# Four stages of a small hybrid decoder on one core: table loads, a gate bank, meta scores and one turn reordered, unused products put into waits

## What the reference computes

```python
u = rmsnorm(h); proj = u @ w_in[l]                 # -> cq 384, ckv 256, kr 32, xr 512, gt 512
q = rmsnorm(rmsnorm(cq) @ w_uq); k, v = rmsnorm(ckv) @ w_ukv ...   # 8 heads, 64 + 32 rotary
att = causal softmax attention                     # blocks of queries: 16 meta, 128, 128
rnn = rglru(conv4(xr)) * gelu(gt)                  # sigmoid gates by w_a, w_i, then a scan
h = h + concat(rmsnorm(att), rmsnorm(rnn)) @ w_out[l]
h = h + (swiglu(rmsnorm(h)) if l == 0 else top-2-of-8 mixture of swiglu experts)
```

## Time and profile before

| what | value |
|---|---|
| median of 3 runs | 895.87 us (894.41 to 896.41) |
| the profiled execution | 898.03 us, its span 896.2 us |
| busy | PE 866.8 us (97%), DVE 683.6, ACT 576.0, POOL 70.8 |
| mean granted clock | 0.985 of full speed |

### The profile page before, as it was taken

How to read it: one execution, slowest core, us unless ns; L and a number is a source line. 1 busy time by engine, 2 the same in 40 slices (tenths; PEclk the granted TensorE clock), 3 DMA queues, 4 the chain that set the end, 5 groups by cost and what they waited for, 6 DMA issues and landing times.

```text
span 896.2 us, 15435 instructions
## 1 busy us (share of the span) xinstructions
PE 866.8 (97%) x5827; PEld 794.5 (89%) x5827; DVE 683.6 (76%) x914; ACT 576.0 (64%) x782; POOL 70.8 (8%) x93
## 2 busy tenths in 40 slices
PE   8989899999999999999899999999999999999995
PEld 7855789999999999965799989999998989999994
DVE  5667867766666555677877889789897998789883
ACT  6666746555454443666746777787778777777762
POOL 3530010000000000000042000000000000000001
PEclk9999899999999999999999999999999999999998
DMA  9505025555578553405055799899998999899981
GB/s 314 189 2 185 17 95 165 173 179 187 167 199 240 144 170 112 142 19 170 13 206 182 261 362 371 324 348 404 345 405 302 372 391 361 314 353 402 353 346 26
DMA packets 119436, 208.70 MB, mean 233 GB/s; under 512 B 5968, under 2 KB 71760, under 8 KB 119376
## 3 DMA queue, kind: packets, MB, share of 16 engines
q1 hardware_dynamic: 117232, 201.79, 63.7%
q0 software_dynamic: 1568, 5.24, 2.9%
q10 hardware_dynamic: 576, 0.87, 0.4%
HBM read 202.65 MB, written 5.24 MB: 232 GB/s over the span
## 4 chain that ended last, share of the span: by engine, by line
PE 85%; DVE 6%; ACT 4%; DMA 3%; issue 2%; POOL 0%; ACTq 0%; DVEq 0%; POOLq 0%; SPq 0%
PE ps L2551 27%; PE ps L2576 12%; PE ps L668 11%; PE ps L670 11%; PE ps L669 10%; PE ps L2156 2%; PE ps L2516 2%; DVE wlo L1436 2%; PE ps L2263 2%; PE ps L2322 1%; DMA raw<-in_w_in_dram 1%; PE ps L2047 1%; PE ps L2563 1%; DMA raw<-in_moe_w_down_dram 1%; DVE rr L1453 1%
## 5 line engine op out<-in xcount | busy, mean ns | idle before, releaser
L1436 DVE TENSOR_TENSOR wlo<-raw,whi 128x1536 fp32r<-128x1536 f32 (+4 forms) x298 | 437.9, 1495 | 90.5 <-ACT whi L984 88.2
L984 ACT ACTIVATE whi<-raw 128x1536 fp32r<-128x1536 f32 (+4 forms) x298 | 374.7, 1275 | 128.6 <-PE ps L670 58.1
L668 PE MATMUL ps<-uhi,whi 128*128 128x272 f32 (+1 forms) x576 | 170.3, 296 | 0.6 <-DVE wlo L1436 0.6
L670 PE MATMUL ps<-uhi,wlo 128*128 128x272 f32 (+1 forms) x576 | 166.8, 290 | 0.0
L669 PE MATMUL ps<-ulo,whi 128*128 128x272 f32 (+1 forms) x576 | 166.5, 289 | 0.0
L2551 PE MATMUL ps<-whi,xeh 128*128 128x320 f32 (+1 forms) x512 | 125.0, 325 | 0.0
L2551 PE MATMUL ps<-whi,xel 128*128 128x320 f32 (+1 forms) x512 | 123.5, 322 | 0.0
L2551 PE MATMUL ps<-wlo,xeh 128*128 128x320 f32 (+1 forms) x512 | 123.5, 322 | 0.0
L668 PEld LDWEIGHTS ps<-uhi,whi 128*128 128x128 f32 (+1 forms) x576 | 109.0, 189 | 4.2 <-issue 2.2
L669 PEld LDWEIGHTS ps<-ulo,whi 128*128 128x128 f32 (+1 forms) x576 | 109.2, 190 | 0.6
L670 PEld LDWEIGHTS ps<-uhi,wlo 128*128 128x128 f32 (+1 forms) x576 | 108.9, 189 | 0.0
(11 more groups left out here) (314 smaller groups left out, 1200.3 us busy)
## 6 DMA issues: line engine op xcount, KB each, us to landing
raw<-in_moe_w_down_dram SPq DMA_DIRECT2D x24, 1536.0 KB, 9.2
raw<-in_moe_w_gate_dram SPq DMA_DIRECT2D x16, 1536.0 KB, 7.5
raw<-in_moe_w_up_dram SPq DMA_DIRECT2D x16, 1536.0 KB, 8.5
raw<-in_moe_w_gate_dram SPq DMA_DIRECT2D x16, 1280.0 KB, 10.1
raw<-in_moe_w_up_dram SPq DMA_DIRECT2D x16, 1280.0 KB, 9.4
raw<-in_ffn_w_gate_dram SPq DMA_DIRECT2D x11, 1024.0 KB, 5.2
raw<-in_ffn_w_up_dram SPq DMA_DIRECT2D x11, 1024.0 KB, 5.2
raw<-in_ffn_w_down_dram SPq DMA_DIRECT2D x8, 1408.0 KB, 6.9
```

The source lines that it names most:

```text
L668: pe.matmul(dst, wh, xh, start=start, stop=False, skip_group_check=True)
L670: return pe.matmul(dst, wl, xh, start=False, stop=stop, skip_group_check=True)
L984: act.activation(placed(whi, s, src), src, ACT.Copy).then_inc(hi_done, 1)
L1436: dve.tensor_tensor(placed(wlo, s, src), src, placed(whi, s, src).bitcast(F32), ALU.subtract).then_inc(lo_done, 1)
```

## The change

- Layer 1's gate block 3 gets bank 5, which was bank 7. Layer 0 keeps its banks.
- ACT's `tables()` and `mark(ACT.Tanh)` stand at the end of step xr 2, which was step xr 1.
- The meta scores of layer 0 go into one bank (6) as eight products side by side. DVE adds the mask, scales, takes the maximum and subtracts it, each for all heads in one instruction. ACT does one exponential for all heads, and `averages(0)` sums them on DVE. TensorE waits for the bank of gt 2 (bank 4) and puts two unused 128 x 128 products into it before heads 2, 4 and 6. Gate block 2 overwrites them.
- Three unused products stand before TensorE's wait at the query scales (`qrt`), in both layers, and the wait for the bank is ahead of them.
- In routing there are three unused products before the wait for `sel_done`, one before the wait for the norm, and two between the last two blocks of `hidden_state`. They go into bank 1.
- In the last expert DVE makes the low parts of the second turn between pieces 18 and 19. ACT's order stays as it was.

```diff
-GT_BANK = (6, 5, 4, 7)
+GT_BANK = ((6, 5, 4, 7), (6, 5, 4, 5))
...
-                for h in range(NH):
-                    add("s", t, h)
+                for h in range(NH if t else 1):
+                    add("s", t, h, bank=None if t else 6)
...
-                    if (name, c) == ("xr", 1):
+                    if (name, c) == ("xr", 2):
                         if not l:
                             tables()
                         mark(ACT.Tanh)
...
+                    if not t:
+                        s = scores[0][0:NMETA, :, 0:NMETA]
+                        act.activation(s, s, ACT.Exp).then_inc(exp_done, NH)
+                        return
...
+                def meta_maxima():
...
+                    dve.wait_ge(filled, b.ready())
+                    dve.tensor_tensor(s, ps[0:n, b.bank, 0:NH * n].rearrange("p (h k) -> p h k", h=NH), mask, ALU.add)                       .then_inc(emptied[b.bank], 1)
+                    dve.wait_ge(emptied[b.bank], b.before + 1)
+                    link(dve.tensor_tensor(s, s, of_head(rt[0:n, 0, :]), ALU.mult))
+                    link(dve.tensor_reduce(small[0:n, 0, 0, :], s, AX.X, ALU.max))
+                    dve.tensor_tensor(s, s, of_head(small[0:n, 0, 0, :]), ALU.subtract).then_inc(sc_done, 1)
...
+                    if not t:
+                        link(dve.tensor_reduce(small[0:n, 0, 2, :], scores[0][0:n, :, 0:n], AX.X, ALU.add))
...
-                    w(e, p, 18, 19)
-                    turned(6, TURN_B, 2)
+                    if is_last(e):
+                        w(e, p, 18)
+                        turned(6, TURN_B, 2)
+                        w(e, p, 19)
+                    else:
+                        w(e, p, 18, 19)
+                        turned(6, TURN_B, 2)
...
-                pe.wait_ge(rows_done, ROWS_DONE[l, "qk"])
                 b = B[l, "qrt"]
                 fill(pe, b)
+                for _ in range(3):
+                    pe.matmul(ps[:, b.bank, 0:P], ident, ident, start=True, stop=True, skip_group_check=True)
+                pe.wait_ge(rows_done, ROWS_DONE[l, "qk"])
...
+                def meta_scores():
...
+                    fill(pe, b)
+                    fill(pe, B[l, "gt", 2])
+                    for h in range(NH):
+                        if h in (2, 4, 6):
+                            unused(B[l, "gt", 2].bank, 2)
+                        kb = B[l, "kbc", h]
+                        pe.wait_ge(emptied[kb.bank], kb.before + 1)
+                        q = pe.matmul(ps[0:n, b.bank, n * h:n * (h + 1)], qT[0:QKH, h, 0:n], kT[0:QKH, h, 0:n],
+                                      start=True, stop=True)
+                    q.then_inc(filled, 1)
...
+            pe.wait_ge(emptied[spare.bank], spare.before + 1)
+            unused(3)
             pe.wait_ge(sel_done, 1)
...
+            unused(1)
             pe.wait_ge(nsum_done, KD - 2)
...
             hidden_state(0, 1)
+            unused(2)
             hidden_state(1, 1)
```

More of the change, by code:

```diff
@@ L260, in plan_blocks @@
             if what == "scores":
-                for h in range(NH):
-                    add("s", t, h)
+                for h in range(NH if t else 1):
+                    add("s", t, h, bank=None if t else 6)
             elif what == "gt":
-                add("gt", t, bank=GT_BANK[t])
+                add("gt", t, bank=GT_BANK[l][t])
             elif what == "meta":
@@ L1588, in _, with of_head @@
                 dve.wait_ge(qscale_done, l + 1)
+                def meta_maxima():
+                    n = NMETA
+                    m0 = C_MASK + T - P
+                    b = B[l, "s", 0, 0]
+                    s = scores[0][0:n, :, 0:n]
+                    mask = con[0:n, m0:m0 + n].rearrange("p (h k) -> p h k", h=1).to_broadcast([n, NH, n])
+                    def of_head(row):
+                        return row.rearrange("p (h k) -> p h k", k=1).to_broadcast([n, NH, n])
+                    dve.wait_ge(filled, b.ready())
[4 more added lines that the diff above has]
+                    dve.tensor_tensor(s, s, of_head(small[0:n, 0, 0, :]), ALU.subtract).then_inc(sc_done, 1)
                 def maxima(t):
                     lead, n = TILES[t]
+                    if not t:
+                        return meta_maxima()
                     keys = lead + n
@@ L2253, in _, with unused @@
                 pe.wait_ge(qrot_done, l + 1)
+                def meta_scores():
+                    n = NMETA
+                    b = B[l, "s", 0, 0]
+                    fill(pe, b)
[8 more added lines that the diff above has]
+                    q.then_inc(filled, 1)
+                def unused(bank, n):
+                    for _ in range(n):
+                        pe.matmul(ps[:, bank, 0:P], ident, ident, start=True, stop=True, skip_group_check=True)
                 def score(t):
                     lead, n = TILES[t]
+                    if not t:
+                        return meta_scores()
                     for h in range(NH):
@@ L2470, in hidden_state, with unused @@
                 q.then_inc(filled, 1)
+            spare = B[1, "wo", 5]
+            def unused(n):
+                for _ in range(n):
+                    pe.matmul(ps[:, spare.bank, 0:P], ident, ident, start=True, stop=True, skip_group_check=True)
             hidden_state(0, 0)
```

## The result

The changed kernel takes 887.98 us (median of 4 runs, 885.65 to 888.30) against 896.14 us before (4 runs beside it, 894.41 to 899.51): 8.2 us faster. The ratio, which is estimated from the single runs and not from the two medians, is 0.9890 (95% interval 0.9852 to 0.9928, which is 6.5 to 13.3 us). In a second comparison, some time later, it was 888.44 against 896.79 us, ratio 0.9919 (0.9897 to 0.9942). The profiled execution took 887.85 us, its span is 886.0 us, its mean granted clock 0.991.

The account below looks back on a forecast made before the run. TensorE, busy 97%, was taken as the bound, with time to win only in its idle, half-clock or off-chain places. Terms (a) to (h) summed to 9.0 us, off the median 895.87: 886.9 us, range 883.7 to 891.6.

Parts of the forecast that it names:

- (a): Layer 0 input stage: root ahead of the table loads, so DVE starts the reciprocal without its 1.79 us idle; 1.8 us won.
- (b): Layer 0, reciprocal to first query product: TensorE's gap shrinks to about 1.0 us and its clock stays up; 1.5 us won.
- (c): Recurrence gates, both layers: ACT's table load goes and TensorE closes its 1.07 us gap; 1.07 us each, 2.1 together.
- (e): Meta scores of layer 0: DVE starts later, but the tiles run at full clock; 0.7 us won, otherwise 0.8 lost.
- (g): Routing: gathers pushed back 0.6 us but taking 4.3 us at full clock; 0.4 us won, otherwise 0.6 to 1.2 lost.
- (h): Last expert's second turn: new DVE order wins 0.95 us, and the clock kept behind a 1.5 us gap 1.6; 2.55 together.
- (d): Query scales, both layers: three unused products take 0.7 us in a wait of 0.72; 0.1 us lost, bounds 0 and 1.4.
- (f): Gate block 3's bank, layer 1: TensorE's wait moves behind two transposes; value 0, bounds 0.3 us won and 1 lost.
- Unused products don't hold the clock: Rival: the clock falls at meta scores and routing, and behind the last turn's gap; gain 4.85 us, 891.0; chance 0.26.
- Transfers set the pace: Rival: the experts' transfers set their pace, earlier gains are lost and 2.55 us stay; 893.3 us; chance 0.07.
- A table load is put back: Rival: a load returns before the gates or the root, losing (c), or (a) with (b); 889 to 890.2 us; chance 0.06.
- Slower at half clock: Rival: unused products run at half clock and lengthen the path by 5.4 us; 896.4 to 897.7 us; chance 0.04.

Follow-up runs that it names:

- tables back: Changed kernel with the tables and tanh mark back at the end of step xr 1: 894.10 us, ratio to before 0.9966.
- no unused: Changed kernel without its 3 + 6 + 6 unused products, waits and banks kept: 890.29 us, ratio 0.9901.
- only tables: Kernel before with only the tanh mark and table work moved behind input block xr 2 instead of xr 1: 890.66 us, ratio 0.9925.

## Why the prediction was right, point by point

The forecast was 886.9 us and 9.0 us of gain; measured 887.98 and 8.2. What repeats in every profile makes 2.0 (a) + 1.5 (b) + 2.7 (c) + 0.3 (e) + 1.3 (g) + 0.7 (h) = 8.5 us: the gain of the medians, 8.2 and 8.35, without any of the stages that vary.

That the total came so close is in part luck. Without the clock of (h) the sum had 7.35 us, so these parts gave 1.15 more: (c) and (g) were 1.4 us too low, (e) and (h) 0.7 too high. The remaining 1.6 us of the forecast were a term that comes true in about half of the profiles. The causes of (a), (b) and (c), three quarters of the gain, were as said, and experiments in both directions show them.

(a) *Root of layer 0.* Predicted 1.8. The stage is 18.3 to 18.9 us in the twelve profiles with the new order, mean 18.64, against 20.64 before and 20.41 in "tables back": 2.0 or 1.8. DVE has no idle time, as said. Of the margin of POOL's softplus, a microsecond by my guess, nothing is left: ACT waits 0.17 us at 57.24. It costs nothing, since the stage around it is 23.13 us in both layers.

(b) *Clock.* Predicted 1.5, measured 1.51. The gap came out at 0.79 us, not 1.0, and the clock is 1.00.

(c) *Loads at the gates.* Predicted 1.07 each, measured 1.34 and 1.35. I took the gap alone. The two groups of eight took 2.10 us each, the sixteen in one piece 3.94: 2 × 2.10 + 1.07 - 3.94 = 1.33. So a gap cost some 0.26 us beside its own length; no run tells what these are made of. The Trainium skill ("ScalarE: Activation LUTs", "What ACT_TABLE_LOAD costs") has a larger price, about 2.7 us for a switch of which 1.38 are a drain. The drain doesn't show here on either side of a load: the split ends at 41.13, the load begins at 41.16, and the sine begins 0.01 us after its end. The page doesn't say on which side the drain lies; "after" was my reading.

(d) *Query scales.* Predicted 0.1 lost in all; measured nothing: the stage is 5.10 us before and 5.10 and 5.09 after. Only against "no unused" (5.17 and 5.18) are 0.07 us won in each layer.

(e) *Meta scores.* Predicted 0.7, measured 0.27. The four DVE operations took 1.14 us (I had 1.3) and the tiles came at full clock. But TensorE's part is dearer, and DVE starts 1.56 us later, not 0.85. From TensorE's first meta product to DVE's start it is 1.27 us without unused products (80.83 to 82.10), where I had 0.8, and 2.88 with six, so 0.27 each in place of 0.23. The argument that the clock falls without them was right for one profile of four with the new scores and no unused products: the shorter meta scores alone mostly did what I put down to the unused ones.

(f) *Gate bank.* Predicted 0, bounds 0.3 won and 1 lost. The first value product does start where it did, 7.60 us behind the gate's next step. The first profile pair shows 1.18 lost; over all profiles no price is shown, and one inside the bound of 1 not excluded.

(g) *Routing.* Predicted 0.4, measured 1.26. The gathers are pushed back 0.15 us, not 0.6: the products lie for the most part in waits that TensorE has anyway. And they take 4.05 us, not 4.3.

(h) *Last expert.* Predicted 0.95 for the order, measured 0.66: the turn's low parts end 0.76 us behind the end of ACT's high parts (865.95 to 866.71), where I had 0.5, and TensorE follows 0.09 later. Predicted 1.6 for the clock, with a gap of 1.5 us; the gap is 1.89, and the clock held in the first profile and fell in the second. This term was a draw, 1.55 or 0, with the gap just where both happen. Of the 0.4 us by which the gap is longer than I said, 0.3 are what the order fell short of, and 0.1 the landing of piece 19; over the profiles with the new order the landing alone moved the gap between 0.92 and 2.21 us.

The rivals. "Unused products don't hold the clock" was wrong for routing, and right for the last turn in four of the eight profiles with the new order and an unfilled wait. "Transfers set the pace" fell: what was won ahead of the experts is still there at their end but for 0.7 us, and their stage lasts 379.5 to 381.8 us with no link to an edit. Transfers do set the landing of the last pieces, and with it the gap of (h): in the chain of waits that step lasts 7.98 us before, 7.07 in "tables back" and 8.88 in "only tables". "A table load is put back" fell. "Slower at half clock" fell: 6.1 us of the gain never touch an unused product.

Two stages flattered the first pair of profiles. Their spans differ by 10.2 us, 2 us more than the medians. 1.55 us are the draw of (h). 1.71 us lie before the first norm root, where no part of the change reaches: TensorE's first products took 0.43 us each in the profile of before and 0.28 in that of after. All thirteen other profiles have 21.9 to 22.3 us there, "only tables" too; with one profile of before it stays open whether that is usual for it.

Open is also what decides, at equal products and equal gaps, whether the clock falls. No run varied that by itself.

## What to carry to other kernels

Look for activation functions whose table is in place and move them ahead of a load, above all where the other engines wait for them: that was 6 of 8 us here, and cost one line. Closing a gap on TensorE gave back its own length and 0.26 us more. Fill a wait with unused products only where it is on the path, the products fit into it, and the clock behind it is seen to fall in more than one profile; where they lengthen the path, as at the meta scores, they are an insurance with a premium of 0.27 us each, and four profiles without them put the average loss below the premium. Look also at which of several waits the products come to stand in: behind the long gap of bank 7 they only added to the path. And before a single stage of one profile is explained, profile the same kernel twice.

## What the runs showed of the hardware

- Behind a gap of 0.65 us on TensorE at the meta scores the granted clock was once 0.50 and three times 1.00; in two of the three the instructions ahead were the same, in the third six unused ones at the query scales were missing. Ahead of the last nine products gaps of 0.92 and 1.23 us left it up, 1.80 to 1.89 us did so twice in five profiles, 2.21 us and more never in four.
- Filling a wait doesn't always keep the clock: in layer 1 the clock fell once behind the filled wait, at the wide value product (2.08 us), and twice at the unused products themselves, which stood behind a gap of 2.40 us (2.99 and 3.22 us for sixteen, against 1.95 at full clock).
- An unused product of 128 columns in fp32, two instructions, took 0.25 us at full clock (twelve instructions in 1.50 us), and 0.27 to 0.31 where it stood between short score products.
- The experts' stage of 380 us varies by 2.3 us between profiles, all of it in the landing of the last pieces: the first 368.5 us, with the DMA engines 96 to 97% busy, agree within 0.25 us in fourteen profiles.
